# Both heads' probabilities transposed in one group and copied by one 1024-column operation in the two-head attentions

## The chip, the cores and the metric

The kernel runs on one core of one Trainium2 chip. The metric is the device time of one execution in microseconds (us), from the first to the last instruction of the program with what lies around them; lower is better. Times are given as the median of several executions.

## The reference, cut to what matters

The program is a stack of four transformer blocks over 512 tokens with 1024 features, all in float32. The first two blocks (DEPTH = 2) each hold two attentions of eight heads of width 64, and these four attentions are what the change touches. In each of them every head has a 512x512 matrix of probabilities:

```
# A: global attention, 8 query heads on 2 key heads, with a norm and a rotation of q and k
s = jnp.einsum('bqkgd,bskd->bkgqs', qi, k).astype(jnp.float32)
p = jax.nn.softmax(s, axis=-1)
return jnp.einsum('bkgqs,bskd->bqkgd', p.astype(v.dtype), v)

# C: neighbourhood attention; computed here as a full 512x512 score matrix
# with a table added that holds the bias inside the window and -1e30 outside of it
s = s + bias.astype(jnp.float32)[None]
p = jax.nn.softmax(s.reshape(B, C_HEADS, GRID_W, win_r * NA_COLS), axis=-1)
return jnp.einsum('bhqrj,brqjhd->bqhd', p, v_nb)
```

The rest (projections, a gated merge, a convolution module, a dilated attention called D here, and four gated feed-forward blocks) is matrix products of 512 tokens with large weights, and is not touched.

## The kernel before

Every engine has its own program, written out by hand in order, and the engines meet through semaphores that only count up. TensorE (PE) does the products and transposes, VectorE (DVE) the maxima and divisions, ScalarE (ACT) the exponentials and copies out of PSUM, GpSimd (POOL) loads and prepares tables, and SyncE (SP) streams the weights.

An attention of kind C or A is cut into 32 steps: a step is one head and one block of 128 queries, against all 512 keys. Steps 2j and 2j+1 are a pair: the two heads that share a 128-row tile, for the same block of queries. There are 16 pairs, four for each two heads. In what follows j is the number of the pair, and these are the pieces of it:

- scores(j) on TensorE (L1691 in C, L1767 in A): both heads' 128x512 scores, into PSUM banks 0 and 1 or 6 and 7.
- negated_max on VectorE (L1193 with the table added, or L1264; then L1041): one for each step. It counts `maxed` up.
- exp on ScalarE (L699): one for each step, with the row sum read out. It counts `probs` up.
- divide on VectorE (L1031, L1033): the reciprocal of the sum, then the 128x512 probabilities times it, in SBUF. It counts `scaled` up.
- turn_probs on TensorE (L1622): four 128x128 transposes of one step's probabilities, into PSUM bank 2 (even step) or bank 3 (odd step). It counts `turned` up.
- copy on ScalarE (L706): 128x512 from that bank into SBUF (`gain`, four slots). It counts `pt_ready` up.
- weigh on TensorE (L1658): eight products of both heads' transposed probabilities with the values. It counts `weighted` up.

After every fourth pair y_round on ScalarE (L731) and y_rest on VectorE (L1082) take the finished 128x512 output tile. In A, four times (pairs 3, 7, 11 and 15) a product of the pooling branch is put in between: L1776 on TensorE, L834 on ScalarE, L1268 on VectorE.

The probabilities lie in three slots (SLOTS = 3). The order on each engine, in the loop over j, is:

- TensorE: scores(j+1), transposes of step 2j, weigh(j-1), transposes of step 2j+1.
- ScalarE: copy of step 2j-1, y_round if due, copy of step 2j, exp of 2j+2, exp of 2j+3, pooling if due.
- VectorE: divide 2j+1, maxima of 2j+2 and 2j+3, divide 2j+2, pooling or y_rest if due.

In C the tables of biases are prepared by GpSimd (L514 loads, L519 adds a mask, 128x1792) for the third and the fourth two heads while the attention runs; the loads are let go when the maxima of the first, then of the second eight steps are done. Behind each C attention TensorE goes on with projections (first_a), behind each A attention with the merge, which waits for the last y_rest.

Of the kernel before, what the change touches and what calls it, by code (L numbers as in the profile page):

```python
# [22 lines left out]
ACT = mybir.ActivationFunctionType  # L23
# [3 lines left out]
T = 512  # L27
# [117 lines left out]
def build(nc, A, out):  # L145
    with ExitStack() as ctx:
# [13 lines left out]
        gain = sb("gain", 2 * D)  # L160
# [58 lines left out]
        def bank(b, n=1):  # L219
            return ps[:, b * T:(b + n) * T]  # L220
# [131 lines left out]
        def turned_probs(g):  # L352

            return gain[:, (g % 4) * T:(g % 4 + 1) * T]
# [222 lines left out]
        def _(act):  # L577
            ch = Chain(act, act_self)
            sc = nc.scalar
# [110 lines left out]
            def pair_attention(kind, n0, pbuf, extra):  # L690

                def exp(n):
                    g = n0 + n
                    s, q = g % SLOTS, g % 4
                    act.wait_ge(maxed, g + 1)
                    if n >= SLOTS:
                        act.wait_ge(turned, g - SLOTS + 1)
                    p = pbuf[:, s * T:(s + 1) * T]
                    sc.activation(p, p if kind == "C" else score_bank(n), ACT.Exp, bias=small[:, q:q + 1],  # L699
                                  scale=rq[:, n:n + 1] if kind == "A" else 1.0, accum_out=small[:, 8 + q:9 + q]).then_inc(probs, 1)  # L700

                def copy(n):
                    act.wait_ge(turned, n0 + n + 1)
                    if n >= 4:
                        act.wait_ge(weighted, n0 + 2 * (n // 2) - 2)
                    sc.activation(turned_probs(n0 + n), bank(2 + n % 2), ACT.Copy).then_inc(pt_ready, 1)  # L706

                exp(0)
                exp(1)
                if 0 in extra:  # L710
                    extra[0]()
                for j in range(18):
                    if 1 <= j <= 16:
                        copy(2 * j - 1)
                    if j >= 5 and (j - 5) % 4 == 0:
                        y_round(n0, (j - 5) // 4, 8 if kind == "C" else 0)
                    if j < 16:
                        copy(2 * j)
                    if j < 15:
                        exp(2 * j + 2)  # L720
                        exp(2 * j + 3)
                    if j and j in extra:
                        extra[j]()
# [190 lines left out]
        def _(dve):  # L914
# [142 lines left out]
            def pair_attention(n0, pbuf, scores_in, scale, pair_out, extra):  # L1057

                negated_max(n0, 0, scores_in, scale)
                negated_max(n0, 1, scores_in, scale)  # L1060
                divide(n0, pbuf, T)
                for j in range(18):
                    if j < 16:
                        divide(n0 + 2 * j + 1, pbuf, T)
                    if j == 0 and j in extra:
                        extra[j]()
                    if j < 15:
                        negated_max(n0, 2 * j + 2, scores_in, scale)
                        negated_max(n0, 2 * j + 3, scores_in, scale)
                        divide(n0 + 2 * j + 2, pbuf, T)  # L1070
                    if j and j in extra:
                        extra[j]()
                    if j >= 5 and (j - 5) % 4 == 0:
                        pair_out((j - 5) // 4)
# [85 lines left out]
            for l in range(2):  # L1160
# [17 lines left out]
                for j in range(5):  # L1178
                    qkv_out(j)
                    if l == 0 and j == 1:  # L1180
                        for r in range(3):
                            n = min(4 * P, ROWS_ALL - 4 * r * P)
# [198 lines left out]
            for hp in range(4):  # L1381
# [24 lines left out]
                n0 = STEPS["D"] + 8 * hp  # L1406
# [25 lines left out]
        def _(pe):  # L1432
# [181 lines left out]
            def turn_probs(n0, n, pbuf):  # L1614

                g = n0 + n
                pe.wait_ge(scaled, g + 1)
                if n >= 2:
                    pe.wait_ge(pt_ready, g - 1)
                for j in range(4):  # L1620
                    at = (g % SLOTS) * T + j * P
                    ins = te.transpose(bank(2 + n % 2)[:, j * P:(j + 1) * P], pbuf[:, at:at + P], ident)  # L1622
                ins.then_inc(turned, 1)

            def pair_attention(kind, n0, scores, pbuf, weigh, v_drained=None, behind=None, extra={}):

                for j in range(17):
                    if j < 15:
                        if j:
                            pe.wait_ge(probs if kind == "A" else maxed, n0 + 2 * j)  # L1630
                        scores(j + 1)
                    if j < 16:
                        turn_probs(n0, 2 * j, pbuf)
                    if j in extra:
                        extra[j]()
                    if j == 16 and behind:
                        behind()
                    if j == 1 and v_drained:
                        pe.wait_ge(drained, v_drained)
                    if j:  # L1640
                        pe.wait_ge(pt_ready, n0 + 2 * j)
                        weigh(j - 1)
                    if j < 16:
                        turn_probs(n0, 2 * j + 1, pbuf)

            def weigh_pair(kind, l, vbuf):

# [17 lines left out]
            for l in range(2):  # L1665
                c, d = FIRST[f"c_qkv{l}"], DRAINS[f"c_qkv{l}"]
                first_two(c, f"pre{2 * l}") if l else first_two_of_all()
                if l == 0:
                    pe.wait_ge(init_in, 16 * len(param_loads))
                    for r in range(3):  # L1670
                        if r == 2:
                            pe.wait_ge(drained, 2 + d + 1)
                        for j in range(min(4, ROW_TILES - 4 * r)):
                            n = 4 * r + j
# [273 lines left out]
```

## Time and profile before

| what | value |
|---|---|
| device time, median of 3 | 3412.98 us (3412.93 to 3414.3) |
| device time of the profiled execution | 3412.23 us |
| its span, first to last instruction | 3410.4 us |
| TensorE matmul busy | 3254.4 us, 95% |
| VectorE busy | 1780.0 us, 52% |
| ScalarE busy | 1237.5 us, 36% |
| first and last transpose of attention C, block 1 | 94.16 and 158.42 us |
| of attention A, block 1 | 234.94 and 292.83 us |
| of attention C, block 2 | 987.75 and 1051.06 us |
| of attention A, block 2 | 1127.57 and 1185.46 us |

The profile has a page of sums and a trace that can be asked for stretches: a timeline of one engine's instructions in order of time, and a table of busy time by window. A timeline row gives the start in us, the length in us, the engine, the line of the kernel, the operation, what it writes and reads, the shapes and a count where several were merged; a bracket gives how long the engine was idle before it and which instruction released it. PEld is the loading of weights into TensorE, which runs beside the matmuls. The granted clock of TensorE (PEclk) is 1.00 at 2.4 GHz and 0.50 at 1.2 GHz. From first to last transpose the four attentions take 243 us of the 3410.

### The profile page before, as it was taken

Reading aid. Unit: us, or ns where it says so; the run is one execution under the profiler, and the core shown is the slowest. Engines: PE = TensorE matmul, PEld = TensorE weight load, DVE = VectorE, ACT = ScalarE, POOL = GpSimd, SP = SyncE. Lnnn points to the kernel's source line nnn. Section 1 sums busy time; section 2 is a strip of 40 time slices with the busy share of each in tenths; the row PEclk is TensorE's granted clock in tenths of the full one; section 3 lists DMA queues with packets and bytes.
Section 4 is the critical chain, followed back from the end, with each engine's and each line's share of the span. In section 5 each row is a group of like instructions: output and inputs, shape, how many; then the busy total and the mean of one; then the engine's idle time right before and its main releaser. Section 6 shows DMA issues by size and latency. Waiting matters only on the chain.

```text
span 3410.4 us, 41633 instructions
## 1 busy us (share of the span) xinstructions
PE 3254.4 (95%) x16677; PEld 2660.3 (78%) x16677; DVE 1780.0 (52%) x2348; ACT 1237.5 (36%) x1676; POOL 136.8 (4%) x148
## 2 busy tenths in 40 slices
PE   8899999999999899999999988999899999999999
PEld 7566888888877588888887657888788888888887
DVE  4655445553465734555527956553434424555543
ACT  3544224443334622444324234442322212243432
POOL 1130000000020300000000010000000000000000
PEclk9999999999999999999999999999999999999999
DMA  6221322322341123223232112223231221223322
GB/s 162 47 72 50 99 93 92 98 92 93 93 104 55 36 88 98 87 99 98 93 104 64 60 44 91 94 92 105 68 106 59 65 87 62 75 81 98 98 86 87
DMA packets 231696, 288.16 MB, mean 84 GB/s; under 512 B 5397, under 2 KB 188717, under 8 KB 231565
## 3 DMA queue, kind: packets, MB, share of 16 engines
q1 hardware_dynamic: 225628, 266.89, 24.2%
q0 software_dynamic: 5936, 19.40, 2.6%
q8 instruction: 96, 1.57, 0.2%
q14 instruction: 36, 0.29, 0.0%
HBM read 284.18 MB, written 2.10 MB: 84 GB/s over the span
## 4 chain that ended last, share of the span: by engine, by line
PE 86%; DVE 8%; ACT 3%; issue 3%; POOL 0%; DMA 0%; DVEq 0%; ACTq 0%; POOLq 0%
PE ps L1437 18%; PE ps L1439 18%; PE ps L1438 18%; PE ps L1553 6%; PE ps L1554 6%; PE ps L1555 6%; PE ps L1474 2%; PE ps L1476 2%; PE ps L1475 2%; PE ps L1813 2%; PE ps L1622 1%; ACT t_whi L588 1%; PE ps L1658 1%; DVE t_wlo L925 1%; PE ps L1907 1%
## 5 line engine op out<-in xcount | busy, mean ns | idle before, releaser
L925 DVE TENSOR_TENSOR t_wlo<-t_wraw,t_whi 128x2048 fp32r<-128x2048 f32 x252 | 582.4, 2311 | 1349.3 <-ACT t_whi L588 1349.3
L588 ACT ACTIVATE t_whi<-t_wraw 128x2048 fp32r<-128x2048 f32 x252 | 482.7, 1916 | 1498.3 <-PE ps L1439 1009.4
L1437 PE MATMUL ps<-t_hh,t_whi 128*128 128x512 f32 (+1 forms) x2640 | 988.9, 375 | 34.2 <-DVE t_hl L995 25.6
L1439 PE MATMUL ps<-t_hh,t_wlo 128*128 128x512 f32 (+1 forms) x2640 | 980.6, 371 | 0.0
L1438 PE MATMUL ps<-t_hl,t_whi 128*128 128x512 f32 (+1 forms) x2640 | 980.4, 371 | 0.0
L1437 PEld LDWEIGHTS ps<-t_hh,t_whi 128*128 128x128 f32 x2640 | 501.9, 190 | 125.9 <-issue 23.7
L1438 PEld LDWEIGHTS ps<-t_hl,t_whi 128*128 128x128 f32 x2640 | 501.7, 190 | 86.7 <-issue 2.9
L1439 PEld LDWEIGHTS ps<-t_hh,t_wlo 128*128 128x128 f32 x2640 | 501.5, 190 | 84.4
L1555 PE MATMUL ps<-t_whi,t_midl 128*128 128x512 f32 x704 | 273.9, 389 | 0.0
L1553 PE MATMUL ps<-t_whi,t_midh 128*128 128x512 f32 x704 | 273.9, 389 | 0.0
L1554 PE MATMUL ps<-t_wlo,t_midh 128*128 128x512 f32 x704 | 273.9, 389 | 0.0
L1553 PEld LDWEIGHTS ps<-t_whi,t_midh 128*128 128x128 f32 x704 | 132.1, 188 | 27.5
L1554 PEld LDWEIGHTS ps<-t_wlo,t_midh 128*128 128x128 f32 x704 | 132.1, 188 | 27.5
L1555 PEld LDWEIGHTS ps<-t_whi,t_midl 128*128 128x128 f32 x704 | 132.1, 188 | 27.3
L1474 PE MATMUL ps<-t_whi,t_hh 128*128 128x256 f32 x512 | 145.7, 285 | 0.0
L1475 PE MATMUL ps<-t_wlo,t_hh 128*128 128x256 f32 x512 | 144.9, 283 | 0.0
L1476 PE MATMUL ps<-t_whi,t_hl 128*128 128x256 f32 x512 | 144.9, 283 | 0.0
L1105 DVE SCALAR_TENSOR_TENSOR t_accg<-ps,t_pvec,t_accg 128x511 f32<-128x511 f32 (+1 forms) x176 | 119.4, 741 | 0.0
L1105 DVE SCALAR_TENSOR_TENSOR t_accv<-ps,t_pvec,t_accv 128x511 f32<-128x511 f32 (+1 forms) x176 | 119.4, 741 | 0.0
L1361 DVE SCALAR_TENSOR_TENSOR t_vb<-t_ub,t_pvec,t_vb 128x512 f32<-128x512 f32 x160 | 106.4, 748 | 0.0
L762 ACT ACTIVATE t_accg<-t_accg 128x512 f32<-128x512 f32 x88 | 55.7, 633 | 128.1 <-DVE t_accg L1105 127.0
L1474 PEld LDWEIGHTS ps<-t_whi,t_hh 128*128 128x128 f32 x512 | 98.2, 192 | 1.9 <-issue 1.5
(258 smaller groups left out, 3971.4 us busy)
## 6 DMA issues: line engine op xcount, KB each, us to landing
t_wraw<-in_w_in_dram SPq DMA_DIRECT2D x46, 1024.0 KB, 5.3
t_wraw<-in_w_up_dram SPq DMA_DIRECT2D x44, 1024.0 KB, 5.1
t_wraw<-in_ffn_w_in_dram SPq DMA_DIRECT2D x44, 1024.0 KB, 5.1
t_wraw<-in_w_kv_dram SPq DMA_DIRECT2D x24, 1024.0 KB, 5.2
t_wraw<-in_w_down_dram SPq DMA_DIRECT2D x20, 1024.0 KB, 5.0
t_wraw<-in_ffn_w_out_dram SPq DMA_DIRECT2D x20, 1024.0 KB, 5.0
t_wraw<-in_w_branch_dram SPq DMA_DIRECT2D x12, 1024.0 KB, 5.0
t_wraw<-in_w_q_dram SPq DMA_DIRECT2D x12, 1024.0 KB, 5.1
```

Source lines behind the costliest of these rows:

```text
L588: sc.activation(whi[slot][:, :], wraw[slot][:, :], ACT.Copy).then_inc(w_hi, 1)
L925: v.tensor_tensor(wlo[slot][:, :], wraw[slot][:, :], whi[slot][:, :].bitcast(F32), ALU.subtract).then_inc(w_lo, 1)
L1105: ins = v.scalar_tensor_tensor(out=tile(acc, m)[:, o0:o1], in0=from_bank(s, m)[:, i0:i1], scalar=col(cw, r), in1=tile(acc, m)[:, o0:o1], o ...
L1437: te.matmul(out, wh, xh, start=first, stop=False)
L1438: te.matmul(out, wh, xl, start=False, stop=False)
L1439: return te.matmul(out, wl, xh, start=False, stop=last)
L1474: te.matmul(o, xs[0], wh, start=k == 0, stop=False)
L1475: te.matmul(o, xs[0], wl, start=False, stop=False)
L1476: ins = te.matmul(o, xs[1], wh, start=False, stop=k == KT - 1)
L1553: te.matmul(o, xh, wh, start=k == 0, stop=False)
L1554: te.matmul(o, xh, wl, start=False, stop=False)
L1555: ins = te.matmul(o, xl, wh, start=False, stop=k == last)
```

## The change

In all four attentions (the helper pair_attention of each engine and turn_probs):

- TensorE: the transposes of both steps of a pair stand together, ahead of weigh(j-1). The transposes of pair j wait until both copies of pair j-1 are done, where each step waited for the copy out of its own bank.
- ScalarE: one 1024-column copy of PSUM banks 2 and 3 (copy_two) takes the place of two 512-column copies. It waits for the transposes of both steps, and stands ahead of y_round and of the two exponentials.
- VectorE: the divide of step 2j+3 comes ahead of the pooling or y_rest of pair j, not behind it. All else there keeps its order.

```
-                def copy(n):
-                    act.wait_ge(turned, n0 + n + 1)
-                    if n >= 4:
-                        act.wait_ge(weighted, n0 + 2 * (n // 2) - 2)
-                    sc.activation(turned_probs(n0 + n), bank(2 + n % 2), ACT.Copy).then_inc(pt_ready, 1)
+                def copy_two(j):
+                    act.wait_ge(turned, n0 + 2 * j + 2)
+                    if j >= 2:
+                        act.wait_ge(weighted, n0 + 2 * j - 2)
+                    sc.activation(gain[:, 2 * (j % 2) * T:2 * (j % 2 + 1) * T], bank(2, 2), ACT.Copy).then_inc(pt_ready, 2)
...
                 for j in range(18):
-                    if 1 <= j <= 16:
-                        copy(2 * j - 1)
+                    if j < 16:
+                        copy_two(j)
                     if j >= 5 and (j - 5) % 4 == 0:
                         y_round(n0, (j - 5) // 4, 8 if kind == "C" else 0)
-                    if j < 16:
-                        copy(2 * j)
                     if j < 15:
                         exp(2 * j + 2)
                         exp(2 * j + 3)
...
                 divide(n0, pbuf, T)
+                divide(n0 + 1, pbuf, T)
                 for j in range(18):
-                    if j < 16:
-                        divide(n0 + 2 * j + 1, pbuf, T)
...
                         divide(n0 + 2 * j + 2, pbuf, T)
+                        divide(n0 + 2 * j + 3, pbuf, T)
...
                 if n >= 2:
-                    pe.wait_ge(pt_ready, g - 1)
+                    pe.wait_ge(pt_ready, n0 + 2 * (n // 2))
...
                     if j < 16:
                         turn_probs(n0, 2 * j, pbuf)
+                        turn_probs(n0, 2 * j + 1, pbuf)
...
                     if j:
                         pe.wait_ge(pt_ready, n0 + 2 * j)
                         weigh(j - 1)
-                    if j < 16:
-                        turn_probs(n0, 2 * j + 1, pbuf)
```

TensorE's order for one pair of attention C before: L1691 are scores, L1622 transposes, L1658 weigh.

```order
L1691 MATMUL ps<-t_kC,t_qC 128x512 [waits maxed]
L1691 MATMUL ps<-t_kC,t_qC 128x512
L1622 MATMUL ps<-t_base,t_pC 128x128 [waits pt_ready,scaled]
L1622 MATMUL ps<-t_base,t_pC 128x128 x3
L1658 MATMUL ps<-t_gain,t_vC 64x128 [waits pt_ready]
L1658 MATMUL ps<-t_gain,t_vC 64x128 x7
L1622 MATMUL ps<-t_base,t_pC 128x128 [waits pt_ready,scaled]
L1622 MATMUL ps<-t_base,t_pC 128x128 x3
```

The same place now, where the lines are L1688, L1620 and L1655.

```order
L1688 MATMUL ps<-t_kC,t_qC 128x512 [waits maxed]
L1688 MATMUL ps<-t_kC,t_qC 128x512
L1620 MATMUL ps<-t_base,t_pC 128x128 [waits pt_ready,scaled]
L1620 MATMUL ps<-t_base,t_pC 128x128 x3
L1620 MATMUL ps<-t_base,t_pC 128x128 [waits pt_ready,scaled]
L1620 MATMUL ps<-t_base,t_pC 128x128 x3
L1655 MATMUL ps<-t_gain,t_vC 64x128 [waits pt_ready]
L1655 MATMUL ps<-t_gain,t_vC 64x128 x7
```

The second group of transposes has moved ahead of weigh, with its two waits.

ScalarE's order around the first y_round (L731) of attention C before: L699 are exponentials, L706 copies.

```order
L699 ACTIVATE t_pC,t_small<-t_pC,t_small 128x512 [waits turned,maxed] x2
L706 ACTIVATE t_gain<-ps 128x512 [waits weighted,turned]
L731 ACTIVATE t_yh<-ps 128x512 [waits weighted]
L706 ACTIVATE t_gain<-ps 128x512 [waits weighted,turned]
L699 ACTIVATE t_pC,t_small<-t_pC,t_small 128x512 [waits turned,maxed] x2
L706 ACTIVATE t_gain<-ps 128x512 [waits weighted,turned] x2
```

The same place now, where y_round is L729.

```order
L699 ACTIVATE t_pC,t_small<-t_pC,t_small 128x512 [waits turned,maxed] x2
L706 ACTIVATE t_gain<-ps 128x1024 [waits weighted,turned]
L729 ACTIVATE t_yh<-ps 128x512 [waits weighted]
L699 ACTIVATE t_pC,t_small<-t_pC,t_small 128x512 [waits turned,maxed] x2
L706 ACTIVATE t_gain<-ps 128x1024 [waits weighted,turned]
```

Both exponentials of the next pair now stand behind one copy that needs the transposes of both steps of this pair.

## Rows read from the trace of the kernel before

**Rows 1.** Timeline of TensorE, attention C of block 1, in its steady part

```profile
128.52 0.66 PE L1622 MATMUL ps<-t_base,t_pC 128*128 128x128 f32 x4
...
130.13 0.66 PE L1622 MATMUL ps<-t_base,t_pC 128*128 128x128 f32 x4
...
131.78 0.44 PE L1622 MATMUL ps<-t_base,t_pC 128*128 128x128 f32 x2
```

**Rows 2.** Timeline of ScalarE, the same place: a copy, an exponential, copy, y_round

```profile
129.21 0.60 ACT L706 ACTIVATE t_gain<-ps 128x512 f32<-128x512 f32 x1 [0.17 <-PE ps L1622]
...
130.99 0.72 ACT L699 ACTIVATE t_pC<-t_pC,t_small 128x512 f32<-128x512 f32 x1
...
131.71 0.58 ACT L706 ACTIVATE t_gain<-ps 128x512 f32<-128x512 f32 x1
132.19 0.58 ACT L731 ACTIVATE t_yh<-ps 128x512 fp32r<-128x512 f32 x1
```

**Rows 3.** Timeline of VectorE, the same place: from maxima to maxima

```profile
129.19 0.68 DVE L1193 CUSTOM_DVE_ANT_0 t_pC<-ps,t_e 128x512 f32<-128x512 f32 x1
...
131.84 0.16 DVE L1031 RECIPROCAL t_small<-t_small 128x1 f32<-128x1 f32 x1 [0.20 <-ACT t_pC L699]
...
132.04 0.49 DVE L1033 TENSOR_SCALAR t_pC<-t_pC,t_small 128x512 f32<-128x512 f32 x1
...
132.44 0.68 DVE L1193 CUSTOM_DVE_ANT_0 t_pC<-ps,t_e 128x512 f32<-128x512 f32 x1
```

**Rows 4.** Timelines of ScalarE, VectorE and TensorE, attention A of block 1

```profile
252.04 0.78 ACT L699 ACTIVATE t_pA<-ps,t_small,t_rq 128x512 f32<-128x512 f32 x1 [0.82 <-DVE t_small L1041]
...
252.89 0.78 ACT L699 ACTIVATE t_pA<-ps,t_small,t_rq 128x512 f32<-128x512 f32 x1
...
252.95 0.16 DVE L1031 RECIPROCAL t_small<-t_small 128x1 f32<-128x1 f32 x1
...
253.15 0.49 DVE L1033 TENSOR_SCALAR t_pA<-t_pA,t_small 128x512 f32<-128x512 f32 x1
...
253.69 0.55 PE L1622 MATMUL ps<-t_base,t_pA 128*128 128x128 f32 x3 [0.42 <-DVE t_pA L1033]
```

**Rows 5.** Timeline of ScalarE: a 1024-column copy out of PSUM, and what follows

```profile
215.05 1.01 ACT L825 ACTIVATE t_pu<-ps 128x1024 f32<-128x1024 f32 x1
215.96 0.28 ACT L829 ACTIVATE t_rq<-ps,t_small 128x32 f32<-128x32 f32 x1
```

**Rows 6.** Timeline of TensorE, attentions A: transposes of step 3, of step 31, last weigh

```profile
240.01 0.66 PE L1622 MATMUL ps<-t_base,t_pA 128*128 128x128 f32 x4
...
292.83 0.66 PE L1622 MATMUL ps<-t_base,t_pA 128*128 128x128 f32 x4
...
294.17 1.09 PE L1658 MATMUL ps<-t_gain,t_vA 128*64 128x128 f32 x16 [0.69 <-ACT t_gain L706]
```

**Rows 7.** Timeline of TensorE, attentions C: transposes of steps 5 and 31, both blocks

```profile
107.50 0.66 PE L1622 MATMUL ps<-t_base,t_pC 128*128 128x128 f32 x4
...
158.42 0.66 PE L1622 MATMUL ps<-t_base,t_pC 128*128 128x128 f32 x4
...
1001.48 0.66 PE L1622 MATMUL ps<-t_base,t_pC 128*128 128x128 f32 x4
...
1051.06 0.66 PE L1622 MATMUL ps<-t_base,t_pC 128*128 128x128 f32 x4
```

**Rows 8.** Timelines of GpSimd and VectorE: the mask added, and a divide beside it

```profile
118.53 3.98 POOL L519 TENSOR_TENSOR t_e<-t_e,t_cmask 128x1792 f32<-128x1792 f32 x1 [7.19 <-DMA t_e<-in_rpbp_dram]
...
119.08 3.71 DVE L1033 TENSOR_SCALAR t_pC<-t_pC,t_small 128x512 f32<-128x512 f32 x1
```

**Rows 9.** Busy time by window, granted clock: header, half clock in C, attention D

```profile
core 0: us, PE busy (x) PEld busy (x) DVE busy (x) ACT busy (x) POOL busy (x), PEclk, DMA share, GB/s
...
138.80:145.70 6.90, 6.26 (x30) 3.77 (x31) 5.83 (x20) 4.11 (x10) 0.30 (x1) 0.51 0.01 4
...
2562.00:2580.00 18.00, 14.35 (x102) 11.79 (x101) 15.31 (x27) 8.88 (x14) 0.00 (x0) 1.00 0.19 60
```

## The prediction, made before the changed kernel had run

> **What bounds the kernel now.** I read the page first (TensorE 95% busy, ScalarE 36%), then the timelines of the four attentions engine by engine, then the busy time by window. Outside of the attentions nothing of the change acts, so the question is how long a pair takes in them, and what closes the loop from one pair to the next.
>
> In attention C the even transposes start at 128.52 and again at 131.78: 3.26 us for a pair, with the odd ones 1.61 behind the even ones [rows 1]. TensorE's four pieces fill that time one behind another: TensorE is the bound there. VectorE has hardly more room: maxima start at 129.19 and again at 132.44, a loop of 3.25, closed by the wait for an exponential at 131.84 [rows 3]. So before, two loops of nearly equal length run, and ScalarE has room in both, since one copy stands ahead of the two exponentials and the other behind them: an exponential never waits for the transposes of the pair's second step. In attention A the pairs are longer: from step 3 to step 31 there are 14 pairs in 52.82 us, 3.77 each [rows 6].
>
> **The change: the new loop.** On ScalarE, exp(2j+2) and exp(2j+3) now stand behind a copy that waits for the transposes of step 2j+1. Those transposes need the divide of step 2j+1, and that needs exp(2j+1), the last instruction of the pair before on ScalarE. So every pair hangs on the last by one chain with no side way. Its links, each with its row:
>
> - Transposes' start to the copy's start: 129.21 - 128.52 = 0.69 [rows 1, 2].
> - The copy's start to the next instruction on ScalarE. A 1024-column copy out of PSUM before: 215.96 - 215.05 = 0.91 [rows 5]. The bounds are 0.48 (a 512-column copy [rows 2], 131.71 to 132.19) and 1.01 (the whole record of the 1024-column one). I take 0.91, the same operation of the same width.
> - First exponential to the second: 0.72 in C (131.71 - 130.99, an exponential and what follows it [rows 2]), 0.85 in A (252.89 - 252.04 [rows 4]).
> - Second exponential to its reciprocal: 0.85 in C (131.84 - 130.99 [rows 2, 3]), 0.91 in A (252.95 - 252.04 [rows 4]).
> - Reciprocal to the division: 0.20 [rows 3, 4].
> - Division to the transposes, where TensorE waited for it: 253.69 - 253.15 = 0.54 [rows 4].
>
> The sum is 0.69 + 0.91 + 0.72 + 0.85 + 0.20 + 0.54 = **3.91 us in C** and 0.69 + 0.91 + 0.85 + 0.91 + 0.20 + 0.54 = **4.10 us in A**. Both are longer than the loops of TensorE (3.26) and VectorE (3.25), so the chain decides, and TensorE waits 0.65 in each pair of C.
>
> What else lies in that chain: y_round stands between the copy and the exponentials now. It is due behind pairs 5, 9 and 13 and holds ScalarE for 0.48 each (as the 512-column copy ahead of it does [rows 2]): 1.44 an attention. The pooling in A stands behind the exponentials on ScalarE, where it has the 1.6 us until the next transposes as cover, and behind both divides on VectorE, where the maxima it pushes are not needed before the copy is done. It costs nothing now; if that cover were 0.7 short it would be 0.7 in three pairs. y_rest is hidden in the same way.
>
> **Attention A.** From step 3 to step 31: 14 x 4.10 + 1.44 = 58.84, against 52.82 before [rows 6]: +6.0. Step 3 itself comes where it does now, since nothing of the old interleaving held it. Behind step 31 there is now weigh(14), which used to be ahead of it, and the last weigh, on which the merge waits, comes later by its length, 1.1 [rows 6]. That is +7.1 for one, and +14.2 for both: the tables' first and last transposes are 57.89 apart in either block.
>
> **Attention C.** From step 5 to step 31 there are 13 pairs: 13 x 3.91 + 1.44 = 52.3. To this comes GpSimd. Its 3.98 us addition of the mask stops a divide beside it: one of usually 0.49 took 3.71 [rows 8], 3.2 lost, and this happens twice in each C attention. The bounds for one are 0 and 3.2 again. Carried forward by the chain, the addition should start some 0.7 behind the transposes of step 11; the next divide is 0.69 + 0.91 + 0.48 + 0.85 + 0.20 = 3.1 behind them, so that 2.4 of the 3.98 have passed, and the second divide of that pair, the one on the chain, comes 1.2 late. I take 1.2, so 2.4 an attention, and 54.7 in all. Before it was 158.42 - 107.50 = 50.92 and 1051.06 - 1001.48 = 49.58 [rows 7], which hold the longer stops and stretches at half the clock (0.51 from 138.8 to 145.7 [rows 9]). The differences are +3.8 and +5.1. Step 5 comes about 1.1 earlier, as no weigh stands between steps 4 and 5, and the projections behind come 1.1 later by weigh(14); these cancel. C together: +8.9.
>
> **The sum.** 14.2 + 8.9 = 23.1. The profiled execution had 3412.23, so it would have 3435.3; the median was 0.75 above it: **3436 us**, 0.7% slower. What is saved (64 copies' starts, 0.05 of ScalarE's time a pair: 2 x 0.48 against 0.91) lies on an engine that only waits less for it.
>
> The Trainium skill has rules for both sides of this, in Perfetto Trace Analysis, section Optimizing Scalar/DVE Operations: grouping into larger operations helps if the engine is saturated, and where it is not saturated but makes others wait, breaking instructions up may let work be done sooner. ScalarE is 36% busy here, so the second one applies, and it speaks against the change. By the first one the sum would be at most 64 x 0.05 = 3 us less than before.
>
> **Rivals.**
>
> *Half clock.* TensorE would be idle for a sixth of each pair, and it did fall to 1.2 GHz behind a stop of 2.7 us in C [rows 9]. At half the clock its 3.26 us of work for a pair is at most 6.5, or 2.5 more than the chain. If a quarter of the 54 pairs went so, that is 14 x 2.5 = +34: 3470. Against it: attention D holds 1.00 for 18 us with TensorE 14.35 of them, or 80%, busy [rows 9], and the new pairs would have 80 to 84%. The Trainium skill (TensorE: Matmul & The Clock Gate, Part 4) says that transposes do not count as busy for the clock in the way that other products do; by that rule this rival would be likelier, but before, with as many transposes, the clock is full through the steady pairs.
>
> *Faster: the chain is shorter than its links.* If ScalarE's copy and the hand-overs overlap more than these rows show, the loop of VectorE is the next floor: 3.25 in C [rows 3], some 3.3 in A, where the old waits for the pooling are gone, too. Then A is 14 x 3.3 = 46.2 + 1.1, or 5.5 less than before, and C is 13 x 3.25 + 2.4 = 44.7, 6.2 and 4.9 less: 3412 - 22 = 3390. It decides from where the chain is 23.1 / 54 = 0.43 shorter than I make it. One link would have to be half of what its row shows, and each was read where its engine waited for it or ran straight on. Little speaks for it.
>
> *About the same.* The chain is 0.3 to 0.55 shorter, with GpSimd's stops all hidden: 3405 to 3419, about 3413.
>
> **How the numbers follow.** The forecast has 0.80, half clock 0.08, about the same 0.06, faster 0.06. The measurement can tell about 0.2% (7 us) from no change; slower is the forecast and half clock, 0.88. The forecast's own ends: low, 0.1 less in the chain (-5.4) and GpSimd's four stops free (-4.8), 3425; high, the copy at its whole 1.01 (+5.4), the stops at 3.2 each (+8.0) and one stretch at half clock in two attentions (+5), 3454. With both open ends that leaves about 2 in 10 out: **3424 to 3454**.
>
> **What would show it.** Right: the odd transposes of C 3.9 apart and those of A 4.1; the copy 1.0 long, with idle time ahead of it released by TensorE in nearly each pair; TensorE idle ahead of transposes, released by the divide. Wrong in the chain: a period under 3.6. Wrong in the stops: a divide of 3.7 us again, and steps 5 to 31 of C over 58 us. Half clock: a granted clock under 0.9 over the steady pairs. Whatever the sum, a change of a microsecond outside of the attentions would be something that I haven't seen.

## The result, and the profile after

| | before | changed |
|---|---|---|
| device time, median | 3412.95 us (3411.12 to 3414.3, 4 runs) | **3441.15 us** (3439.09 to 3444.15, 4 runs) |
| ratio, 95% interval | 1 | **1.0084** (1.0066 to 1.0101) |
| span of the profiled execution | 3410.4 us | 3442.3 us |

The change costs 28.2 us by the medians, 31.9 by the two profiled spans; the profiled execution of the changed kernel is the slowest of its four, 3.0 above their median. The forecast was 3436, its range 3424 to 3454. ScalarE's and TensorE's sums on the page answer to the 36% and 95% before:

```profile
span 3442.3 us, 41521 instructions
...
PE 3264.9 (95%) x16677; PEld 2664.7 (77%) x16677; DVE 1773.5 (52%) x2348; ACT 1224.4 (36%) x1612; POOL 136.6 (4%) x148
```

ScalarE works 13.1 us less (1237.5 before, by the lengths of the records, which overlap), and the program takes 28 us more. The sums don't show why; the order does.

**Attention C**, where [rows 1 to 3] had a pair in 3.26. Timeline of TensorE in the changed kernel (start, length, instruction, idle time before it and its releaser):

```profile
109.47 1.36 PE L1620 MATMUL ps<-t_base,t_pC 128*128 128x128 f32 x8 [0.50 <-DVE t_pC L1031]
110.76 1.09 PE L1655 MATMUL ps<-t_gain,t_vC 128*64 128x128 f32 x16
111.79 1.13 PE L1688 MATMUL ps<-t_kC,t_qC 64*128 64x512 f32 x4
113.42 1.36 PE L1620 MATMUL ps<-t_base,t_pC 128*128 128x128 f32 x8 [0.50 <-DVE t_pC L1031]
```

The same place on ScalarE: copy, two exponentials, copy, y_round, exponential.

```profile
114.86 1.02 ACT L706 ACTIVATE t_gain<-ps 128x1024 f32<-128x1024 f32 x1 [1.52 <-issue]
115.78 0.71 ACT L699 ACTIVATE t_pC<-t_pC,t_small 128x512 f32<-128x512 f32 x1
...
116.49 0.71 ACT L699 ACTIVATE t_pC<-t_pC,t_small 128x512 f32<-128x512 f32 x1
...
118.80 1.02 ACT L706 ACTIVATE t_gain<-ps 128x1024 f32<-128x1024 f32 x1 [1.52 <-issue]
119.72 0.59 ACT L729 ACTIVATE t_yh<-ps 128x512 fp32r<-128x512 f32 x1
120.20 0.72 ACT L699 ACTIVATE t_pC<-t_pC,t_small 128x512 f32<-128x512 f32 x1
```

And VectorE's two divides between those copies:

```profile
116.62 0.16 DVE L1029 RECIPROCAL t_small<-t_small 128x1 f32<-128x1 f32 x1 [0.88 <-ACT t_pC L699]
...
117.32 0.16 DVE L1029 RECIPROCAL t_small<-t_small 128x1 f32<-128x1 f32 x1
117.52 0.49 DVE L1031 TENSOR_SCALAR t_pC<-t_pC,t_small 128x512 f32<-128x512 f32 x1
```

This is the loop of the prediction, read off once around. Copy at 114.86, exponentials at 115.78 and 116.49, the second's reciprocal at 117.32, its division at 117.52, the next copy at 118.80: 0.92 + 0.71 + 0.83 + 0.20 + 1.28 = 3.94. Copies and transposes (109.47, 113.42) both repeat every 3.94 or 3.95. Of that 0.50 is TensorE waiting ahead of the transposes for a division. Another 0.29 lies between their two halves, by experiment 2 (below), where the next instruction starts 1.00 behind the eight transposes that nothing holds up (111.27 to 112.27) and not 1.29 (109.47 to 110.76). The remaining 3.15 is work. Where y_round is due, it adds 119.72 to 120.20, or 0.48.

The copy's idle 1.52 carries the name "issue". Its neighbours say what it is: the transposes end at 113.42 + 1.36 = 114.78, and the copy starts 0.08 behind.

**Attention A**, for [rows 4 to 6]. ScalarE across a pooling step (L832):

```profile
255.91 1.02 ACT L706 ACTIVATE t_gain<-ps 128x1024 f32<-128x1024 f32 x1 [1.52 <-issue]
...
258.34 0.69 ACT L832 ACTIVATE t_yh<-ps,t_pvec 128x512 fp32r<-128x512 f32 x1
259.98 1.02 ACT L706 ACTIVATE t_gain<-ps 128x1024 f32<-128x1024 f32 x1 [0.94 <-issue]
```

259.98 - 255.91 = 4.07 with the pooling in it, and the copy still waits 0.94 behind it: the pooling lies in idle time.

**Where the time lies.** Start of the first step's to start of the last step's transposes in each attention, from the two traces. Here, and wherever periods are given below, the start is that of the weight load (PEld) of the first of the four transposes; the row of the product itself begins at most 0.1 us or so later.

| | C, block 1 | A, block 1 | C, block 2 | A, block 2 | sum | rest of the span |
|---|---|---|---|---|---|---|
| before | 64.26 | 57.89 | 63.30 | 57.88 | 243.3 | 3167.1 |
| changed | 67.90 | 65.65 | 70.14 | 65.41 | 269.1 | 3173.2 |
| difference | +3.6 | +7.8 | +6.8 | +7.5 | **+25.8** | **+6.1** |

**The clock.** Busy time by window in the changed kernel (header, then the start of attention A of block 1, steady pairs of C, steady pairs of A):

```profile
core 0: us, PE busy (x) PEld busy (x) DVE busy (x) ACT busy (x) POOL busy (x), PEclk, DMA share, GB/s
234.00:250.90 16.90, 14.28 (x50) 7.17 (x51) 11.12 (x27) 6.80 (x14) 14.91 (x15) 0.50 0.20 63
...
109.40:117.30 7.90, 6.80 (x56) 3.99 (x56) 5.83 (x21) 4.85 (x11) 1.97 (x3) 1.00 0.82 116
254.40:285.00 30.60, 26.21 (x208) 15.34 (x208) 23.54 (x62) 19.93 (x39) 0.00 (x0) 1.00 0.01 1
```

The steady pairs hold 2.4 GHz with TensorE 86% busy. But A of block 1 now starts with 16.9 us at 1.2 GHz, behind a wait of 5.28 us for the keys and queries. The wait isn't new. Timeline of TensorE there, in the kernel before and in the changed one:

```profile
230.25 3.79 PE L1767 MATMUL ps<-t_kA,t_qA 64*128 64x512 f32 x8 [5.27 <-DVE t_small L1261]
```

```profile
234.98 3.78 PE L1764 MATMUL ps<-t_kA,t_qA 64*128 64x512 f32 x8 [5.28 <-DVE t_small L1259]
...
244.30 2.31 PE L1620 MATMUL ps<-t_base,t_pA 128*128 128x128 f32 x8 [0.65 <-DVE t_pA L1031]
246.54 1.97 PE L1655 MATMUL ps<-t_gain,t_vA 128*64 128x128 f32 x16
248.44 2.08 PE L1764 MATMUL ps<-t_kA,t_qA 64*128 64x512 f32 x4
250.46 0.77 PE L1620 MATMUL ps<-t_base,t_pA 128*128 128x128 f32 x3
```

Before, the clock fell as well, but the full one was back at 234.4, ahead of the first transposes (6.8 us in all); now it is back at 250.9 (17.1 us in all). At 1.2 GHz TensorE's work is the longer loop (250.46 - 244.30 = 6.16 from even to even), and the first two periods of the odd transposes are 4.97 and 5.56 us, not 4.06. The clock isn't the only cause: GpSimd prepares the pooling branch at the same time, and a divide beside it takes 1.49 us, not 0.49.

```profile
248.67 1.27 POOL L554 TENSOR_TENSOR t_pu<-t_win,t_pu 128x512 f32<-128x512 f32 x1
...
248.72 1.49 DVE L1031 TENSOR_SCALAR t_pA<-t_pA,t_small 128x512 f32<-128x512 f32 x1
```

Experiment 9 (below) parts the two. By the granted clock, 114.6 us of the program run at 1.2 GHz, 95.8 before.

**GpSimd's stop**, for [rows 8]: timelines of GpSimd and VectorE.

```profile
118.31 3.99 POOL L519 TENSOR_TENSOR t_e<-t_e,t_cmask 128x1792 f32<-128x1792 f32 x1 [6.94 <-DMA t_e<-in_rpbp_dram]
...
121.24 1.34 DVE L1031 TENSOR_SCALAR t_pC<-t_pC,t_small 128x512 f32<-128x512 f32 x1
```

Most of the 3.99 us now passes while VectorE has nothing to divide; the divide takes 1.34, not 3.71. At the three other stops the slowest divide takes 1.60, 0.89 and 2.26.

### The profile page after: what moved, and what is told of

Its sections match the earlier page's. It is cut to its first block, busy times and chain, and to the rows that moved or that the text cites. A ratio compares the mean times of both kernels' runs of the same rounds, so it can differ in the third digit from the quotient of the medians.

```text
span 3442.3 us, 41521 instructions
## 1 busy us (share of the span) xinstructions
PE 3264.9 (95%) x16677; PEld 2664.7 (77%) x16677; DVE 1773.5 (52%) x2348; ACT 1224.4 (36%) x1612; POOL 136.6 (4%) x148
## 4 chain that ended last, share of the span: by engine, by line
PE 58%; DVE 4%; ACT 2%; issue 1%; POOL 0%; DVEq 0%; POOLq 0%; ACTq 0%
PE ps L1435 12%; PE ps L1436 12%; PE ps L1437 12%; PE ps L1551 5%; PE ps L1552 5%; PE ps L1553 5%; PE ps L1810 1%; PE ps L1474 1%; PE ps L1473 1%; PE ps L1472 1%; PE ps L1904 1%; ACT t_whi L588 1%; DVE t_vb L1359 1%; DVE t_wlo L923 1%; PE ps L1893 1%
## 5 line engine op out<-in xcount | busy, mean ns | idle before, releaser
L706 ACT ACTIVATE t_gain<-ps 128x1024 f32<-128x1024 f32 x64 | 65.5, 1023 | 105.1 <-issue 91.9
```

## Experiments

The theory: every pair hangs on one chain, transposes, wide copy, two exponentials, two divides, because ScalarE takes its instructions in order. The rivals: the grouping on TensorE itself costs the time, or the half clock does. Differences are of medians, against runs of the kernel before on the same chip (3412.2 to 3412.4).

**1. The transposes grouped, but two narrow copies, both ahead of the exponentials.**

```
-                    sc.activation(gain[:, 2 * (j % 2) * T:2 * (j % 2 + 1) * T], bank(2, 2), ACT.Copy).then_inc(pt_ready, 2)
+                    for n in (2 * j, 2 * j + 1):
+                        act.wait_ge(turned, n0 + n + 1)
+                        if n >= 4:
+                            act.wait_ge(weighted, n0 + 2 * (n // 2) - 2)
+                        sc.activation(turned_probs(n0 + n), bank(2 + n % 2), ACT.Copy).then_inc(pt_ready, 1)
```

> The changed kernel with its grouped transposes, but two 512-column copies in place of the wide one, both ahead of the exponentials; the first may start when the even step is transposed. Theory (one chain through the odd step: transposes, copy, two exponentials, divide): the even copy drops out of the chain, the odd one holds it for 0.48 in place of 0.91, so the odd transposes come 3.94 - 0.43 = 3.51 apart in C and 4.06 - 0.43 = 3.63 in A; over 54 pairs -23 us, about 3418. Rival (the cost comes from grouping the transposes on TensorE ahead of the values): periods stay at 3.9 and 4.1, about 3441.

Measured: 3428.43 (3427.07 to 3429.15), ratio 1.0048 (1.0031 to 1.0065). That is +16.0 and so 12.2 less than the change's 28.2, though ScalarE has as many copies as at first. Timeline of ScalarE in C:

```profile
110.67 0.60 ACT L707 ACTIVATE t_gain<-ps 128x512 f32<-128x512 f32 x1 [0.77 <-PE ps L1621]
111.45 0.60 ACT L707 ACTIVATE t_gain<-ps 128x512 f32<-128x512 f32 x1 [0.19 <-PE ps L1621]
111.95 0.71 ACT L699 ACTIVATE t_pC<-t_pC,t_small 128x512 f32<-128x512 f32 x1
```

The first copy now runs beside the second four transposes, and behind them the exponentials wait 0.50 (111.45 to 111.95) instead of 0.92. C's period was 3.47 (3.51 expected). Attention A's was 3.6 to 4.07, where 3.63 was expected. The time came out 10 above the theory's 3418, and the traces put more of that in C than in A. From step 5 to step 31 C is 2.6 and 2.9 us shorter than in the changed kernel, where 13 x 0.43 = 5.6 was expected, and GpSimd's addition now stops a divide for longer at three of the four places: the slowest divides are 2.87, 1.58, 3.17 and 3.03, where they were 1.34, 1.60, 0.89 and 2.26. From step 3 to step 31 A is 5.9 and 4.4 shorter, where 6.0 was expected. The number was missed, the direction held.

**2. The wide copy kept, but behind the exponentials.**

```
                 for j in range(18):
+                    if j < 15:
+                        exp(2 * j + 2)
+                        exp(2 * j + 3)
                     if j < 16:
                         copy_two(j)
                     if j >= 5 and (j - 5) % 4 == 0:
                         y_round(n0, (j - 5) // 4, 8 if kind == "C" else 0)
-                    if j < 15:
-                        exp(2 * j + 2)
-                        exp(2 * j + 3)
```

> The changed kernel, but on ScalarE both exponentials of the next pair stand ahead of the wide copy and y_round, not behind. Theory: the chain is opened, since an exponential no longer waits for the odd transposes through the copy. What is left in A is VectorE's loop, 3.3 us a pair; in C the maxima of the odd step wait for the slot that the even transposes free: 0.69 + 0.92 + 0.72 + 1.07 = 3.4 us a pair. Total 3441 - 54 x 0.6 = about 3405, at or under the kernel before. Rival (grouping the transposes costs by itself): periods 3.9 to 4.1, about 3441.

Measured: 3435.68 (3435.06 to 3437.54), 1.0071 (1.0054 to 1.0088). **The theory missed here**: 3405 was expected. The chain from copy to exponential is cut, and two others took its place. Timeline of TensorE in C, then of VectorE in A:

```profile
111.27 1.07 PE L1620 MATMUL ps<-t_base,t_pC 128*128 128x128 f32 x8 [0.60 <-ACT t_gain L706]
112.27 1.09 PE L1655 MATMUL ps<-t_gain,t_vC 128*64 128x128 f32 x16
...
114.87 1.06 PE L1620 MATMUL ps<-t_base,t_pC 128*128 128x128 f32 x8 [0.45 <-ACT t_gain L706]
```

```profile
265.42 0.69 DVE L1080 TENSOR_TENSOR t_yl<-ps,t_yh 128x512 fp32r<-128x512 f32 x1 [0.71 <-ACT t_yh L729]
...
273.55 0.75 DVE L1266 SCALAR_TENSOR_TENSOR t_yl<-ps,t_pvec,t_yh 128x512 fp32r<-128x512 f32 x1 [0.80 <-ACT t_yh L832]
```

First: eight transposes that fill both banks wait for the copy that empties both (released by ScalarE's copy, not by the divide). The loop is 3.60 in C: transposes, the odd step's maxima (which wait for the slot of probabilities that the transposes free), its exponential, copy, transposes. Second: y_round and the pooling now stand behind a late copy, and VectorE, which stops for them at L1080 and L1266, holds up the maxima behind. Periods of A: 3.97, 4.22, 3.32, 4.72.

**3. VectorE's part alone, on the kernel before.**

```
                 divide(n0, pbuf, T)
+                divide(n0 + 1, pbuf, T)
                 for j in range(18):
-                    if j < 16:
-                        divide(n0 + 2 * j + 1, pbuf, T)
...
                         divide(n0 + 2 * j + 2, pbuf, T)
+                        divide(n0 + 2 * j + 3, pbuf, T)
```

> The kernel before with VectorE's part of the change alone: the divide of step 2j+3 ahead of the pooling and y_rest. Theory: it is a small gain, since in A the divide no longer waits behind the pooling product: the 4.5 us pairs, three in each A attention, lose up to 0.8; 2 x 3 x 0.7 = -4 us, 3409. Rival (VectorE's order is part of what costs): over 3413 by 3 us or more.

Measured: 3414.87 (3411.83 to 3416.85, 10 runs), 1.0007 (0.9997 to 1.0016). No effect that can be measured; 3409 was expected. In the trace each A attention is 0.96 shorter (56.93 and 56.92): three of four periods are 3.26 and the fourth, with the pooling, 4.75. C of block 2 is 2.07 longer (65.37), with 13.7 us at half the clock instead of 10.2.

**4. ScalarE's part alone, nearly: the wide copy kept, the odd transposes back behind weigh.**

```
                     if j < 16:
                         turn_probs(n0, 2 * j, pbuf)
-                        turn_probs(n0, 2 * j + 1, pbuf)
...
                         weigh(j - 1)
+                    if j < 16:
+                        turn_probs(n0, 2 * j + 1, pbuf)
```

> The changed kernel with TensorE's old order: transposes of the odd step behind the values of the pair before, the wide copy kept. Theory: the values, 1.03 us, then stand inside the chain between the even and the odd transposes. The even ones are ready 3.19 behind the last odd ones, so the period is 3.19 + 0.59 + 1.03 = 4.81 in C and 5.0 in A: 54 x 0.9 = +48, about 3490. Rival (grouping costs): the old order on TensorE gives back the loss, about 3413.

Measured: 3527.83 (3526.45 to 3528.41), 1.0338 (1.0321 to 1.0355). Timeline of TensorE in C:

```profile
113.58 0.66 PE L1620 MATMUL ps<-t_base,t_pC 128*128 128x128 f32 x4 [1.52 <-DVE t_pC L1031]
114.16 1.09 PE L1656 MATMUL ps<-t_gain,t_vC 128*64 128x128 f32 x16
115.19 0.66 PE L1620 MATMUL ps<-t_base,t_pC 128*128 128x128 f32 x4
115.77 1.13 PE L1689 MATMUL ps<-t_kC,t_qC 64*128 64x512 f32 x4
118.43 0.66 PE L1620 MATMUL ps<-t_base,t_pC 128*128 128x128 f32 x4 [1.52 <-DVE t_pC L1031]
```

118.43 - 113.58 = 4.85 (4.81 expected), and 4.91 in A (5.0). Weigh now lies inside the chain. So beside a wide copy the grouping doesn't cost, it spares: without it the change costs 115, four times as much. What the grouping would cost with two narrow copies in their old places wasn't run. The 38 us beyond the expected 3490 lie in pairs of 5.3 to 8.8 us. Most of these have stretches at half the clock (169.1 us of the program run at 1.2 GHz, 95.8 before), and in C the longest stand at GpSimd's stops, where a divide takes 2.63 to 3.34 us and TensorE waits 4.13 at 125.88; how much is the clock's part isn't shown. The steady pairs of 4.85 and 4.91, with their waits of 1.5 to 1.6, keep the full clock. C with everything in it is 65% busy:

```profile
105.00:170.00 65.00, 42.11 (x305) 25.87 (x305) 37.71 (x108) 27.68 (x57) 14.40 (x10) 0.88 0.20 29
```

**5. GpSimd's stop taken out of both kernels.** The mask is added to 2 columns only; what is outside of the window isn't masked.

```
-                    gp.tensor_tensor(v, v, m, ALU.add).then_inc(e2_ready, 1)
+                    gp.tensor_tensor(v[:, 0:1, 0:2], v[:, 0:1, 0:2], m[:, 0:1, 0:2], ALU.add).then_inc(e2_ready, 1)
```

On the kernel before: 

> The kernel before, with GpSimd's addition of the mask cut from 1792 columns to 2 (the window's mask is left out, so attention C attends too widely; every other instruction and wait stays). It prices the stops that the addition makes. Theory: in the trace of the kernel before, the pairs at the stops are 3.1 and 5.6 us over the 3.26 of the others in block 1, 3.1 and 4.2 in block 2, so 16 us go and it takes about 3397. If the stops are hidden elsewhere, it stays at 3412.

On the changed kernel: 

> The changed kernel with the same cut (the window's mask is left out). Theory: its stops cost less, since a divide comes later in a pair and the chain leaves VectorE free time: 3.0 us over the period in block 1 and 3.8 in block 2, so 7 us go: 3434. Then the change costs 3434 - 3397 = 37 us where no stop covers a part of it. If the stops cost the same in both kernels, it takes 3425.

Measured: before without stops 3399.48 (3398.58 to 3401.04), 0.9964 (0.9949 to 0.9978); changed without stops 3440.21 (3437.9 to 3442.39), 1.0080 (1.0064 to 1.0097). The stops cost 12.7 us before, while the changed kernel without them still stands 28.0 above the kernel before, and between two kernels without them the change costs 40.7 (37 expected). Stop and chain share their time: the changed loop has idle time on VectorE in which a stop passes. The 6 us by which the changed kernel missed its 3434 aren't in C, which is 1.9 and 3.8 shorter by the trace (66.02, 66.35), but in stretches outside of the attentions; their cause stays open.

**6. The chain opened at each place that experiment 2 had shown.** Exponentials first, then y_round and pooling, then the wide copy; a fourth slot for the probabilities, so that maxima and exponentials don't wait for transposes to free one. Attention D keeps three slots.

```
-SLOTS = 3
+SLOTS = 4
...
-                    if j < 16:
-                        copy_two(j)
-                    if j >= 5 and (j - 5) % 4 == 0:
-                        y_round(n0, (j - 5) // 4, 8 if kind == "C" else 0)
                     if j < 15:
                         exp(2 * j + 2)
                         exp(2 * j + 3)
-                    if j and j in extra:
+                    if j >= 5 and (j - 5) % 4 == 0:
+                        y_round(n0, (j - 5) // 4, 8 if kind == "C" else 0)
+                    if j and j in extra and j < 15:
+                        extra[j]()
+                    if j < 16:
+                        copy_two(j)
+                    if j == 15 and j in extra:
                         extra[j]()
```

> The changed kernel with the chain taken apart, but both transposes still in one group and one 1024-column copy: both exponentials, then y_round or the pooling, then the wide copy; and four slots for the probabilities in place of three in these attentions, so that the maxima of the odd step don't wait for the even transposes. Theory: what is left is TensorE at 3.26 and VectorE at 3.25 in C and 3.3 in A, with 1.3 us of y_rest and pooling in four pairs of A, 3.6; weigh(14) behind the last transposes stays at 1.1 in four places. That is 3412 + 4.4 - 3.6 = about 3413. Rival (grouping or the wide copy costs by itself): 3425 or more.

Measured: 3422.16 (3420.29 to 3423.33, 8 runs), 1.0029 (1.0018 to 1.0039). The sum of the four attentions is 247.4. That is +10.0, so 18.2 of the 28.2 us come back, and 10 stay with wide copy and grouping. The run changes the order on ScalarE and the number of slots together, and a fourth slot alone, in the kernel before, wasn't run: that all of the 18.2 is the chain's is argued, not shown. Timeline of TensorE in A:

```profile
262.22 1.07 PE L1624 MATMUL ps<-t_base,t_pA 128*128 128x128 f32 x8 [0.66 <-ACT t_gain L707]
263.22 1.09 PE L1659 MATMUL ps<-t_gain,t_vA 128*64 128x128 f32 x16
264.24 1.13 PE L1768 MATMUL ps<-t_kA,t_qA 64*128 64x512 f32 x4
265.65 1.07 PE L1624 MATMUL ps<-t_base,t_pA 128*128 128x128 f32 x8 [0.28 <-ACT t_gain L707]
```

What is left in the pairs is, by these waits, the second bank. Before, four transposes filled one bank while the other was being copied out; now both are filled and emptied together. C alternates between 3.25 and 3.61. The attentions' sum is 247.4 - 243.3 = 4.1 us longer; that this is the bank's price is argued from the waits for the copy, since the divide's new place and the fourth slot are in the same sum. The last weigh, now behind all transposes, adds some 1.2 at each attention's end, 4.9 for four: together 9.0 of the 10.

**7. The stop made harmless on the kernel before, with all the work done.** The mask is added in four pieces of 448 columns.

```
-                    gp.tensor_tensor(v, v, m, ALU.add).then_inc(e2_ready, 1)
+                    for part in range(4):
+                        ins = gp.tensor_tensor(v[:, 7 * part:7 * part + 7], v[:, 7 * part:7 * part + 7],
+                                               m[:, 7 * part:7 * part + 7], ALU.add)
+                        ins.then_inc(e2_ready, 1)
...
-                    dve.wait_ge(e2_ready, 4 * l + hp + 1)
+                    dve.wait_ge(e2_ready, 4 * (4 * l + hp + 1))
```

> The kernel before with GpSimd's addition of the mask in four pieces of 448 columns. Theory: a divide is held for the rest of one piece (1.0 us) and gets in between two of them, so a stop costs 1 to 2 us in place of 3.1, and the second one no longer takes the clock down: 2 to 3 us less for each of four, about 3402. If the pieces together hold the divides as long as the whole does: 3412.

Measured: 3402.80 (3399.98 to 3404.37), 0.9971 (0.9959 to 0.9984): faster than both kernels. Timelines of GpSimd, and of two divides beside it:

```profile
120.19 4.80 POOL L520 TENSOR_TENSOR t_e<-t_e,t_cmask 128x448 f32<-128x448 f32 x4 [6.95 <-DMA t_e<-in_rpbp_dram]
...
120.99 0.62 DVE L1036 TENSOR_SCALAR t_pC<-t_pC,t_small 128x512 f32<-128x512 f32 x1
...
124.38 0.90 DVE L1036 TENSOR_SCALAR t_pC<-t_pC,t_small 128x512 f32<-128x512 f32 x1
```

GpSimd takes longer (4.80, not 3.98), and these divides lose 0.13 and 0.41 instead of 3.2; 0.90 is the longest in this run's C attentions. In both kernels the divide ends 0.28 us behind the GpSimd instruction that it met: 122.79 against 122.51 before [rows 8], now 121.61 against 121.33, the end of the first piece, and 125.28 against 125.00, the end of the last. The Trainium skill (SBUF — State Buffer, section Who interferes with whom) says that GpSimd and VectorE, where both need a pair of ports that they share, hold it for a whole instruction, and the other is blocked, not slowed. The trace agrees with that: what decides is the length of a piece, not GpSimd's total.

The stops cost 12.7 us (experiment 5), and the pieces give back 9.4. One pair of 4.87 is left in each C attention. In block 1 the maxima there start at 140.10, right behind the last piece of the mask's addition, which ends at 139.97: they seem to wait for the table itself.

**8. Experiments 3 and 7 together.**

> The kernel before with GpSimd's mask addition in four pieces and VectorE's part of the change (divide of step 2j+3 ahead of pooling and y_rest). Theory: the two gains add: 3403 of the pieces alone less 1 us in each A attention, 3401, which beats both kernels. If the order of the divide costs in C what it gives in A: 3403 to 3405.

Measured: 3401.25 (3399.72 to 3402.8, 7 runs), 0.9969 (0.9957 to 0.9980). The four attentions sum to 231.5 us, 11.9 less than before. Its median is the lowest of all versions that do the whole work, but it can't be told from experiment 7's.

**9. TensorE kept busy ahead of attention A**, in the changed kernel, with ten 512-column products whose results nobody reads, at the place where it waits for the queries.

```
                 pe.wait_ge(head_std, 2 * l + 2)
+                keep_warm(5)
                 pe.wait_ge(qk_ready, 6 * l + 6)
```

> The changed kernel with ten extra products of 512 columns (4.4 us, result unused) on TensorE where it waits 5.3 us ahead of each A attention. Theory on the second loss (TensorE goes into attention A at half the clock and, waiting in each pair, gets the full one back late): the first two intervals of A fall from 4.97 and 5.4 to 5.6 to about 4.2 and 4.1, 2 us in each, so 3437. If the half clock comes from the pairs themselves: first intervals as before, 3441.

Measured: 3441.69 (3441.01 to 3443.15), 1.0088 (1.0074 to 1.0102). Timeline of TensorE, and the window that answers to 234.00:250.90 above:

```profile
230.04 4.45 PE L1480 MATMUL ps<-t_base 128*128 128x512 f32 x10
235.49 1.99 PE L1765 MATMUL ps<-t_kA,t_qA 64*128 64x512 f32 x8 [1.00 <-DVE t_small L1259]
```

```profile
234.00:250.90 16.90, 10.34 (x74) 5.59 (x72) 13.00 (x30) 7.86 (x16) 15.51 (x15) 1.00 0.20 63
```

The half clock is gone, and attention A with the gap ahead of it is 2.1 us shorter (141.26, not 143.40) and 1.9 in block 2. The first two periods are 4.63 and 4.56, where 4.2 and 4.1 were expected and 4.97 and 5.56 stood. So of the 2.4 us that they were too long, the half clock made 1.3; the other 1.1 stay at full clock, where GpSimd's pooling still stretches divides to 1.04, 0.86 and 0.77 us. The median isn't lower (3437 was expected). The profiled span is, by 3.0, but it is compared with the slowest execution of the changed kernel; where the 4 us went in the median isn't shown.

**10. The same on experiment 8's kernel.**

> The version of e8_pieces_and_divide with the same extra products ahead of each A attention. Theory: up to 1 us less in each A attention than without them, 3399 to 3401; if the half clock there was no cost in the old order: 3401 to 3403.

Measured: 3401.34 (3399.54 to 3401.96), 0.9968 (0.9956 to 0.9980), no gain over 3401.25, though the time at 1.2 GHz fell from 94.3 to 61.9 us. The traces show why nothing came back in attention A: it takes 133.4 us with the gap ahead of it, with the extra products and without. The gap is 0.9 shorter, but in block 1 a divide now falls beside GpSimd's last pooling operation ahead of the first product of that branch (240.66 to 241.92). It takes 1.45 us, TensorE waits 1.49 for it, and that period is 5.68, not 4.53. Block 2 has the same divide of 1.45.

## Why the prediction was right, and where its terms were off

**The chain: right, link by link.** 3.91 was forecast for C and 3.94 measured (4.42 with y_round); 4.10 and 4.06 for A (4.55 with y_round). The largest link, the copy's start to the next instruction, was 0.92 for 0.91. TensorE waits 0.79 in a pair (0.50 + 0.29), not 0.65, since its work in grouped order is 3.15 and not 3.26. Three runs bear the chain out. Experiment 4 puts the values into it, and the period grows to 4.85 and 4.91 (4.81 and 5.0 expected). Experiment 1 shortens it by half a copy, and C's period falls to 3.47 (3.51 expected). Experiment 6 opens it, with the wide copy and the grouping kept, and 18.2 of the 28.2 us come back, with the help of a fourth slot that wasn't tried alone. That the copies stand ahead of the exponentials costs with narrow ones, too: in experiment 1 both do, 12.2 come back and 16 stay, in which the grouping has a part that wasn't measured alone.

**y_round at 0.48 and the pooling at nothing: right** [rows 2], as the rows at 119.72 and 258.34 show. Experiment 2 shows the price once the pooling's cover is gone: a pair of 4.72.

**Attention A: 58.84 was forecast from step 3 to step 31, 59.83 and 59.59 measured.** The term that was missing is the start. I took attention A to begin at full clock, since the steady pairs before had it, and I put no stop of GpSimd's there, though it prepares the pooling branch beside the first pairs. 4.97 + 5.56 for two periods instead of 2 x 4.06 is 2.4 us in block 1, 1.3 by the half clock and 1.1 at full clock too (experiment 9); 1.5 of it lie between steps 3 and 31; the period itself, 0.04 shorter than forecast, gave 0.5 back. In block 2 I had also used the 52.82 of block 1, where 52.08 stood. Inside the A attentions the forecast was +12.0 and the trace shows +15.3.

**Attention C: 54.7 was forecast from step 5 to step 31, 55.70 and 57.01 measured.** Thirteen periods of 3.94 and three y_rounds are 52.7, so 3.0 and 4.3 were lost to the stops and what followed them, where 2.4 was forecast; the four places at which a stop falls are 1.2, 1.8, 0.3 and 3.5 longer than such pairs elsewhere, 6.8 in all for 4.8. The first came as forecast (1.2, over two pairs). I had put the second at the same place in the pair; it isn't, and at such a place TensorE also falls to 1.2 GHz for a while, as it did before [rows 9]. Inside the C attentions: +6.7 forecast (8.9, less 1.1 twice), +10.5 measured.

**The rest: +4.4 was forecast, for weigh at each end; +6.1 measured.** Behind the four attentions the gaps grew by 1.2, 2.6, 1.2 and 1.2. In sum the profiled span grew by 31.9 where 23.1 was forecast, and the median by 28.2. Executions of one kernel differ by 3 to 5 us (3439.09 to 3444.15 for the changed one), so the last few microseconds of the sum aren't explained. All three parts came out above their terms, 3.3, 3.8 and 1.7 us: the 3436 was low, and that 3441 lies within the range is the work of the margin for the stops and the clock.

**The rivals.** Faster and about the same both needed a chain shorter by 0.3 or more, and fell with the measured period. The half clock was held off in the steady pairs, as argued from attention D [rows 9]: 1.00, with TensorE 86% busy. It stayed at the starts of the A attentions instead, where it had been before the change as well, but for less time (6.8 us in block 1 before, 17.1 now). In experiment 4 it took hold of more pairs, but not of the steady ones. The Trainium skill (TensorE: Matmul & The Clock Gate, Part 4) has transposes not counting as busy; with 8 of the 28 instructions of a pair transposes, no steady pair of the changed kernel shows a loss. The Trainium skill's rule that breaking instructions up may let work be done sooner, where an engine isn't saturated but makes others wait (Perfetto Trace Analysis, Optimizing Scalar/DVE Operations), agrees with experiment 1 against the changed kernel: 3428.43 against 3441.15.

**What I hadn't seen:** the lost second bank. In the changed kernel the chain is longer than that loop, which hides it. It came to light in experiments 2 and 6, as waits of 0.28 to 0.66 for the copy. So undoing the chain doesn't bring the change to no loss.

## What to carry to other kernels

Before two operations are merged on an engine that takes its instructions in order, write down one loop around through all engines: the merged operation waits for the later of its two inputs, and all that is queued behind it waits as well. Here ScalarE saved 13 us of work at 36% load, and the pair went from 3.26 to 3.94 us. Merging also turns two buffers into one, which shows only when the first loop is gone; and an operation of GpSimd that stops VectorE is better cut into pieces, which was worth 0.3% here.

## What the runs showed of the hardware

- A 512-column copy out of PSUM holds ScalarE for 0.48 to 0.50 us, a 1024-column one for 0.92: merging saves 0.04 to 0.08 us.
- An addition of 3.98 us on GpSimd stops a division of 0.49 on VectorE for 3.2 to 3.3 us (3.67 to 3.81 in the kernel before); in four pieces of together 4.80 us it costs a division 0.13 to 0.41, in experiment 8 up to 0.74 (1.23). Each divide so stopped, beside whole additions and pieces alike, ends 0.28 or 0.29 us behind the end of the GpSimd instruction. The whole stops were worth 12.7 us (experiment 5), of which the pieces return 9.4.
- TensorE fell to 1.2 GHz across the wait of 5.27 or 5.28 us at the start of attention A in both kernels. Before, the full clock was back 4.2 us behind the end of the wait (234.4); in the changed kernel 15.9 us behind it (250.9), with TensorE busy for 14.28 of the 16.9 us from 234.0. Ten products ahead of it kept it at 2.4 GHz, and the total time was the same.
